# State-space scan: rows of summed decays from a DRAM scratch instead of TensorE spreads

## What is computed

```python
acum = jnp.cumsum(loga, axis=2)            # summed decays, per head
tril = jnp.tril(jnp.ones((CHUNK, CHUNK), dtype=bool))[:, :, None, None]
seg = jnp.exp(jnp.where(tril, acum[:, :, :, None] - acum[:, :, None], -jnp.inf))
cb = jnp.einsum('bcign,bcjgn->bcijg', cm, bm)
y_intra = jnp.einsum('bcijgr,bcjgrp->bcigrp', seg * cb[..., None], v)
cdec = jnp.exp(acum)

def step(s, xc):
    bm_c, wgt_c, v_c, al_c, cm_c, cd_c = xc
    y = jnp.einsum('bign,bgrnp->bigrp', cm_c, s) * cd_c[..., None]
    return advance(s, bm_c, wgt_c, v_c, al_c), y
```

## Time and profile before

| | us |
|---|---|
| median of 3 runs | 2179.41 (2177.7 to 2180.89) |
| the profiled execution | 2180.74, its span 2179.0 |
| TensorE busy | 1892.8 (87%) |
| VectorE, ScalarE, GpSimd busy | 801.6, 508.6, 333.6 |
| the scan, as shown below | 440.3 to 536.7 |

### The profile page before, as it was taken

One profiled execution on the slowest core, in us unless ns is written; L12 is line 12 of the kernel. 1 busy time (PEld: TensorE's weight loads), 2 busy tenths in 40 slices (PEclk: granted clock), 3 DMA queues, 4 the chain that ended last, 5 costly groups with the idle time before them and its releaser, 6 DMA issues.

```text
span 2179.0 us, 32920 instructions
## 1 busy us (share of the span) xinstructions
PE 1892.8 (87%) x14024; PEld 1133.5 (52%) x14024; DVE 801.6 (37%) x1427; ACT 508.6 (23%) x1119; POOL 333.6 (15%) x323
## 2 busy tenths in 40 slices
PE   6999989999999989888899999989999976656566
PEld 3874668845875433333236566578887731212112
DVE  3331757655543010000026877667764300000001
ACT  2452321343012100001023323444442100000001
POOL 1431044422320000000013000045540000000000
PEclk9999999999999999999999999999999987888878
DMA  9321051230239999999993433300004699999997
GB/s 385 142 87 77 2 196 78 102 131 1 96 146 394 429 429 427 429 430 430 430 403 133 188 155 117 127 2 2 3 2 184 235 430 429 428 430 429 432 431 294
DMA packets 46690, 528.07 MB, mean 242 GB/s; under 512 B 3409, under 2 KB 7761, under 8 KB 23121
## 3 DMA queue, kind: packets, MB, share of 16 engines
q1 hardware_dynamic: 44784, 522.56, 57.5%
q10 hardware_dynamic: 1760, 3.42, 0.4%
HBM read 524.91 MB, written 1.05 MB: 241 GB/s over the span
## 4 chain that ended last, share of the span: by engine, by line
PE 54%; DMA 28%; DVE 11%; issue 2%; ACT 2%; DVEq 1%; POOLq 1%; POOL 0%; ACTq 0%; PEld 0%; SPq 0%; PEldq 0%
DMA ring<-in_moe_w 27%; PE bank L1442 12%; PE bank L711 8%; PE bank L822 7%; PE bank L1324 4%; PE bank L1257 3%; PE bank L790 3%; DVE x L2285 2%; PE bank L1020 2%; PE bank L1043 2%; DMA ring<-in_mod_w 1%; DVE x L2877 1%; PE bank L965 1%; DVE ring L2414 1%; PE bank L629 1%
## 5 line engine op out<-in xcount | busy, mean ns | idle before, releaser
L1442 PE MATMUL bank<-ring,xgs 128*32 128x512 f32 x2984 | 377.4, 660 | 128.1 <-DMA ring<-in_moe_w 126.8
L1442 PEld LDWEIGHTS bank<-ring,xgs 128*32 128x32 f32 x2984 | 106.8, 120 | 372.3 <-issue 287.1
L1442 PE MATMUL bank<-ring,hT 128*32 128x512 f32 x1488 | 198.9, 689 | 67.5 <-DMA ring<-in_moe_w 67.5
L822 PE MATMUL bank<-hT,ring 128*128 128x256 f32 (+1 forms) x784 | 232.7, 454 | 2.0 <-ACT hT L1612 1.4
L2718 DVE SCALAR_TENSOR_TENSOR x<-bank,modT,x 128x256 f32<-128x256 f32 x96 | 42.4, 480 | 456.9 <-PE bank L1466 456.7
L822 PEld LDWEIGHTS bank<-hT,ring 128*128 128x128 f32 x784 | 146.6, 190 | 82.3 <-issue 66.8
L1442 PEld LDWEIGHTS bank<-ring,hT 128*32 128x32 f32 x1488 | 54.0, 124 | 198.5 <-issue 149.2
L2285 DVE SCALAR_TENSOR_TENSOR x<-gluR,cols,x 128x256 f32<-128x256 f32 x240 | 116.2, 484 | 16.6 <-issue 0.9
L711 PE MATMUL bank<-hT,ring 128*128 128x256 f32 x432 | 99.9, 381 | 4.2 <-ACT ssd_g L1663 2.2
L711 PEld LDWEIGHTS bank<-hT,ring 128*128 128x128 f32 x432 | 81.1, 190 | 18.2 <-issue 6.3
L3109 POOL MEMSET gluR<- 128x3008 f32 x1 | 2.6, 2611 | 500.0 <-DVEq L2728 500.0
(11 more groups left out here) (578 smaller groups left out, 3057.2 us busy)
## 6 DMA issues: line engine op xcount, KB each, us to landing
ring<-in_moe_w SPq DMA_DIRECT2D x56, 4096.0 KB, 22.6
ring<-in_moe_w SPq DMA_DIRECT2D x28, 2048.0 KB, 20.9
ring<-in_moe_w SPq DMA_DIRECT2D x55, 1024.0 KB, 14.6
ring<-in_mod_w SPq DMA_DIRECT2D x12, 4096.0 KB, 13.5
ring<-in_moe_w SPq DMA_DIRECT2D x12, 3072.0 KB, 21.9
ring<-in_cd_w SPq DMA_DIRECT2D x6, 4096.0 KB, 14.1
ring<-in_ab_w SPq DMA_DIRECT2D x5, 4096.0 KB, 19.5
ring<-in_ab_wo SPq DMA_DIRECT2D x2, 4096.0 KB, 13.9
```

The source lines that it names most:

```text
L822: last = mm(ps[p["no"] % 4][:, p["c0"]:T], w[:, k, :], hT[:, k, p["c0"]:T], start=(k == 0), stop=(k == KD - 1))
L1442: last = mm(ps[banks + s][32 * j:32 * j + 32, :], lhs[s][:, 4 * kh + k, 32 * j:32 * j + 32], piece(g, k, j), start=(kh == 0 and k == 0), s ...
```

## The change

The rows of `ac` are written once to a DRAM scratch (`rows_out`), and each row comes back by a DMA whose source repeats it for 128 partitions, straight into the matrix buffer (`decay_rows`; two per pair and direction, on SP's queue, among the weight loads). The spread and mask products and their constants go. So that no exponential overflows where j lies beyond i, the matrices hp = 1 ("far") take |ac_j - ac_i| on ScalarE, and hp = 0 ("near") the minimum with ac_j on VectorE (`bounded`); the mask, now a factor 0 or 1 (`past`), goes into the C-B product, which is kept per direction. The order of matrices is by direction first; TensorE counts `ssd_y` twice a pair, when direction 0 and when direction 1 has been multiplied. The first four broadcast pairs (k = 0, 1) stand in SP's order ahead of the load `about` 4, the other twelve ahead of `mod10` 0.

```diff
+        def rows_out(sp):
+
+            sp.wait_ge(sg("gate_cums"), 1)
+            sp.dma_start(ssd_rows, ac[64:128, :]).then_inc(sg("dram_written"), 16)
+            sp.wait_ge(sg("dram_written"), 16)
+            sp.wait_ge(sg("gate_cums_turned"), 1)
+
+        def decay_rows(sp, k, d):
+
+            if k >= 2:
+                sp.wait_ge(sg("ssd_y"), 2 * k - 3 + d)
+            for hp in range(2):
+                r = 32 * d + 2 * k + hp
+                sp.dma_start(mats[(4 * k + 2 * d + hp) % 8], ssd_rows[r:r + 1, :].broadcast_to([P, T])).then_inc(sg(f"ssd_row{2 * (k % 2) + d}"), 16)
...
+                if (stage, i) == ("about", 4):
+                    rows_out(sp)
+                    for k in range(2):
+                        for d in range(2):
+                            decay_rows(sp, k, d)
+                if (stage, i) == ("mod10", 0):
+                    for k in range(2, 8):
+                        for d in range(2):
+                            decay_rows(sp, k, d)
                 if n >= RING:
                     sp.wait_ge(w_used, n - RING + 1)
                 load_group(sp, n, stage, i)
...
-                for g in range(2):
-                    dve.wait_ge(sg("ssd_cb"), g + 1)
-                    V.tensor_copy(cbs[g], ps[4 + g]).then_inc(sg("ssd_cbm"), 1)
                 dve.wait_ge(sg("gate_cums_turned"), 1)
...
                 V.tensor_tensor(dtw[:, :, :], ps[2][:, 0:256].rearrange("p (t r) -> p t r", t=NT), acT[:, :, :], ALU.subtract).then_inc(sg("gate_gap"), 1)
+                for g in range(2):
+                    for d in range(2):
+                        V.tensor_tensor(cbs[g][d].rearrange("p (t i) -> p t i", t=NT), ps[4 + g].rearrange("p (t i) -> p t i", t=NT),
+                                        past[:, d:d + 1, :].broadcast_to([P, NT, P]), ALU.mult)
                 dve.wait_ge(sg("gate_exps"), 1)
...
             def ssd():
+                act.wait_ge(sg("ssd_weights"), 1)
                 for k in range(8):
-                    for hp in range(2):
-                        for d in range(2):
-                            u, r = 4 * k + 2 * hp + d, 32 * d + 2 * k + hp
-                            act.wait_ge(sg("ssd_bc"), u + 1)
-                            if k >= 2:
-                                act.wait_ge(sg("ssd_y"), k - 1)
-                            for t in range(NT):
-                                last = A_(mats[u % 8][:, t * P:t * P + P], ps[(4, 5, 7)[u % 3]][:, t * P:t * P + P], ACT.Exp,
-                                          bias=nacT[:, t, r:r + 1])
-                            last.then_inc(sg("ssd_decay"), 1)
+                    for d in range(2):
+                        act.wait_ge(sg(f"ssd_row{2 * (k % 2) + d}"), 32 * (k // 2 + 1))
+                        u, r = 4 * k + 2 * d, 32 * d + 2 * k
+                        far, near = [[mats[(u + hp) % 8][:, t * P:t * P + P] for t in range(NT)] for hp in (1, 0)]
+                        for t in range(NT):
+                            A_(far[t], far[t], ACT.Abs, bias=acT[:, t, r + 1:r + 2], scale=-1.0)
+                        act.drain()
+                        for t in range(NT):
+                            last = A_(far[t], far[t], ACT.Exp, bias=albuf[:, t, r + 1:r + 2], scale=-1.0)
+                        last.then_inc(sg("ssd_decay"), 1)
+                        act.wait_ge(sg("ssd_bounded"), 2 * k + d + 1)
+                        for t in range(NT):
+                            last = A_(near[t], near[t], ACT.Exp, bias=nacT[:, t, r:r + 1])
+                        last.then_inc(sg("ssd_decay"), 1)
...
-                def matrices(k, hp):
+                def matrices(k, d):
...
+                    u = 4 * k + 2 * d
+                    for n, hp in enumerate((1, 0)):
+                        dve.wait_ge(sg("ssd_decay"), u + n + 1)
+                        V.tensor_tensor(mats[(u + hp) % 8], mats[(u + hp) % 8], cbs[k // 4][d], ALU.mult).then_inc(sg("ssd_mat"), 1)
+
+                def bounded(k, d):
...
+                    m, r = mats[(4 * k + 2 * d) % 8].rearrange("p (t i) -> p t i", t=NT), 32 * d + 2 * k
+                    dve.wait_ge(sg(f"ssd_row{2 * (k % 2) + d}"), 32 * (k // 2 + 1))
+                    V.tensor_tensor(m, m, acT[:, :, r:r + 1].broadcast_to([P, NT, P]), ALU.min).then_inc(sg("ssd_bounded"), 1)
...
                     if q in (1, 2):
-                        matrices(k + 1, q - 1)
+                        bounded(k + 1, q - 1)
+                    if q == 3:
+                        matrices(k + 1, 0)
+                    if q == 0 and k >= 0:
+                        matrices(k, 1)
                     if z - 1 in SSD_KV:
                         item_scale(SSD_KV[z - 1])
```

More of the change, by code:

```diff
@@ L166, in hybrid_backbone @@
         ones = sb("ones", [P, P])
-        m_far = sb("m_far", [P, 2, P], BF16)
-        identb = sb("identb", [P, P], BF16)
+        past = sb("past", [P, 2, P])
         rst64 = sb("rst64", [P, T])
@@ L324, in sg @@
             return S[name]
+        ssd_rows = nc.dram_tensor("ssd_rows", (64, T), F32, kind="Internal").ap()
         block = ctx.enter_context(nc.Block())
@@ L362, in load_experts @@
             if layer == 0:
-                sp.wait_ge(sg("ssd_y"), 8)
+                sp.wait_ge(sg("ssd_y"), 16)
                 sp.dma_start(early[:, :], part(last, 0, 4096)).then_inc(early_in, 16)
@@ L598, in _ @@
                 sp.dma_start(out.rearrange("(k p) t -> p k t", p=P)[:, 4 * half:4 * half + 4, :],
-                             hT[:, 4 * half:4 * half + 4, SEQ:T]).then_inc(sg("out_written"), 16)
-            sp.wait_ge(sg("out_written"), 32)
+                             hT[:, 4 * half:4 * half + 4, SEQ:T]).then_inc(sg("dram_written"), 16)
+            sp.wait_ge(sg("dram_written"), 48)
         @block.tensor
@@ L960, in outputs @@
                         if kind and t == 0:
-                            pe.wait_ge(sg("ssd_mat"), 4 * k + 2 + kind)
+                            pe.wait_ge(sg("ssd_mat"), 4 * k + 2 * kind)
                         for hp in range(2):
                             half = slice(64 * hp, 64 * hp + 64)
-                            right = mats[(4 * k + 2 * hp + kind - 1) % 8][:, tiles[t]] if kind else dskI[:, 2 * k + hp, :]
+                            right = mats[(4 * k + 2 * kind - 2 + hp) % 8][:, tiles[t]] if kind else dskI[:, 2 * k + hp, :]
                             last = mm(ps[k % 4][half, tiles[t]], xs_t[:, k, t, half], right, start=False, stop=True,
                                       skip_group_check=True, tile_position=(0, 64 * hp))
+                        if n == 7:
+                            last.then_inc(sg("ssd_y"), 1)
                     if q == 3:
@@ L987, in ssd @@
                         square_sum(z - 28)
+                pe.wait_ge(sg("mod_added"), 3)
                 for c in range(4, 7):
@@ L2604, in out_projection_ab @@
                 dve.drain().then_inc(sg("pair_out"), 1)
-                dve.wait_ge(sg("x_again"), 16)
+                dve.wait_ge(consts_in, 96)
                 for v in range(4):
@@ L2795, in over @@
                     return v[:, t, r0:r0 + 8].rearrange("p (c a) -> p c a", a=2).unsqueeze(3).broadcast_to([P, 4, 2, 64])
-                def matrices(k, hp):
+                def matrices(k, d):
                     if k >= 8:
                         return
[L2801 to L2804, removed]
+                    u = 4 * k + 2 * d
[3 more added lines that the diff above has]
+                def bounded(k, d):
+                    if k >= 8:
+                        return
+                    m, r = mats[(4 * k + 2 * d) % 8].rearrange("p (t i) -> p t i", t=NT), 32 * d + 2 * k
+                    dve.wait_ge(sg(f"ssd_row{2 * (k % 2) + d}"), 32 * (k // 2 + 1))
+                    V.tensor_tensor(m, m, acT[:, :, r:r + 1].broadcast_to([P, NT, P]), ALU.min).then_inc(sg("ssd_bounded"), 1)
                 def item_state(v):
@@ L2828, in gate @@
                     dve.wait_ge(sg("ssd_acc"), 6 * (c // 4 + 1))
-                    dve.wait_ge(sg("ssd_y"), c + 1)
+                    dve.wait_ge(sg("ssd_y"), 2 * c + 2)
                     V.tensor_tensor(zmix[:, c, :], zmix[:, c, :], ps[c % 4], ALU.mult).then_inc(sg("ssd_gated"), 1)
@@ L2947, in _ @@
             G.memset(ones[:, :], 1.0)
-            G.memset(identb[:, :], 0.0)
-            G.memset(m_far[:, :, :], 0.0)
+            G.memset(past[:, :, :], 1.0)
             G.memset(m_gla[:, :, :], 1)
@@ L2958, in _ @@
                             pattern=[[-1, P]], channel_multiplier=1)
-            G.affine_select(out=identb[:, :], in_=identb[:, :], compare_op=ALU.not_equal, fill=1.0, base=0,
-                            pattern=[[-1, P]], channel_multiplier=1)
             for d in range(2):
                 sign = 1 - 2 * d
-                G.affine_select(out=m_far[:, d, :], in_=m_far[:, d, :], compare_op=ALU.is_ge, fill=-1e30, base=0,
```

(3 more changed lines are left out.)

11 lines of the change are left out of this document (3 added, 8 removed).

## The result

| | runs | median us | ratio to before (95%) |
|---|---|---|---|
| before | 8 | 2179.27 | |
| changed | 8 | 2186.05 | 1.0026 (1.0017 to 1.0035) |
| changed, second set | 10 | 2184.65 | 1.0021 (1.0012 to 1.0031) |

The forecast was 2168 in a range from 2160.5 to 2177: the sign is wrong, and some 18 us lie between forecast and measurement. The profiled execution took 2181.81 us and is the quickest of its eight; the second profile (2188.53) is the slowest of its ten.

What follows compares the result with a forecast made beforehand. TensorE was taken to pace the scan: 25.6 us removed, less 1.5 start, 5.7 gaps, 1.4 VectorE order and 5.0 followers, gains 12.0. From 2180.74, less 1.3 more, 2167.4, stated as 2168; range 2160.5 to 2177.

Steps and rivals of the forecast that it cites:

- Gaps laid open: Scan's item chain: six gaps after inter products, formerly covered by spread blocks, give back 0.95 us each, 5.7 in all.
- Where the followers overtake TensorE: Scan: TensorE waits at kv(7) 1.5 us, add(6) 1.7 and the squares at z = 28 1.8; together 5.0.
- VectorE. ... Order matters more: VectorE's queue in the scan: added work fits except before item_scale(1), 0.6 us, and beside GpSimd's skip block, 0.8; together 1.4.
- Removed: TensorE in the scan: 16 spread blocks of 1.60 us each disappear, 25.6 us.
- only TensorE and the bare gaps count: Rival for the scan: rows early, ScalarE never behind, gain 18.9 us, time 2160.5; chance 0.12.
- Start: Start of the scan: waiting for GpSimd's weighting and the new first minimum loses 1.0 and 0.5 us, together 1.5.
- ScalarE: Scan: twelve activations per direction and k at 0.27 us plus 0.2 for the drain, 3.5 us, 16 times 56.
- rival 3: ScalarE reloads its table at every Abs/Exp change: 5 us slower, with stalls about 2186; chance 0.09 including other losses.
- Minima: VectorE in the scan: 16 added minima, 0.68 us each or 0.60 back to back, 10 us in all.
- Transfers: Row broadcasts for the scan land 2.9 us from issue, 3.3 a pair; delayed weight loads still arrive before use.
- rival 2: Scan: ScalarE or the row broadcasts bind more, 2172 to 2179 us, moderate case 2173; chance 0.17.
- Masked copies: ssd_gates on VectorE: four copies instead of two stay hidden behind ScalarE's table load; uncovered they would cost 2.4 us.

Runs made afterwards that it cites:

- warm at the start only: Changed kernel plus ident-by-ident products on TensorE only around the modulation row's turn and at steps -2 and 0; 2182.27 us, ratio 0.9996 to before.
- without spreads: Kernel of before with its spread and mask products removed and nothing put in their place (matrices not computed); 2169.03 us, ratio 0.9947 to before.
- fewer ident products: Changed kernel with GpSimd's mixings held, pair 3's gate earlier and fewer gap-filling ident products than that best version; 2170.78 us, ratio 0.9948 to before.

## Why the prediction was wrong

**The step that failed** is the pricing of idle time in "Gaps laid open" and in "Where the followers overtake TensorE". Each gap was priced at its own length, 0.95 us six times and 5.0 at three later places, with the products between at the durations of a kernel whose clock never fell. The experiments show that the gaps also bring TensorE to its lower clock: products that keep it busy inside the same gaps give back 6.9 us alone (0.9986 against 1.0021), and 0.9957 against 1.0002 with the collision gone. The Trainium skill ("TensorE: Matmul & The Clock Gate", section on a second HAM failure mode) describes a kernel that idles briefly between groups of products and goes back and forth between the two clocks; the traces here agree, and I had not weighed it. The profile's sign was there to be read: the earlier trace rows show TensorE busy 93% of the stage, and the forecast itself put it at 64 of 84 us.

**The second step** is "VectorE. ... Order matters more". The walk met GpSimd's skip block and charged 0.8, but it did not look for what else GpSimd does while the matrices move to later steps. The mixings ran from 507.6 before as well, beside no multiplication of matrices. Their price was 3.9 us alone (1.0002 against 1.0021), and 0.9957 against 0.9986 with the clock held. The Trainium skill ("SBUF — State Buffer", section "SBUF: two separate sides") says that VectorE with two SBUF inputs and GpSimd share a port pair as an exclusive lock held for an instruction, so that the other blocks. The trace agrees: each mixing took about 2.8 us, so the first ended near 507.5, and the multiplication of 2.84 us that began at 505.24 ended at 508.08, some 0.6 behind it.

Of the 18 us between forecast and measurement these two steps hold about 14. With both held, the kernel gains 9 to 10 us against the 12.0 of the sum, and its scan takes 89.8 us where the walk gives 524.7 - 438.8 = 85.9. The rest of the working, term by term:

- *Removed:* 25.6 us of products are gone, as counted. But removal alone shortens the scan by 9.0 us, so "only TensorE and the bare gaps count" was never near. TensorE is busy 76.1 us in the changed scan and not near 64, since part of its products ran at the lower clock.
- *Start:* the first kv product comes 2.59 us behind the copy's start instead of 3.20; 0.6 gained as worked out, and given back by the clock (1.63 us for 1.10).
- *Gaps:* the six that were priced at 0.95 measured 0.87, 1.92, 0.85, 0.94, 5.12 and 0.85 us (steps 0, 4, 8, 17, 21, 25): four as said, one behind GpSimd's skip block (1.0 more, priced at 0.8 under VectorE), one behind the mixings. Steps 15 and 23 had a bare gap before as well, which the forecast does not name; no term hangs on it.
- *ScalarE:* no table load stands between Abs and Exp; rival 3's mechanism is out, though its sign came true. The three sets of four, timeline of ScalarE:

```profile
484.56 1.26 ACT L2005 ACTIVATE x<-x,ssd_g 128x128 f32<-128x128 f32 x4
485.89 1.28 ACT L2008 ACTIVATE x<-x,ssd_g 128x128 f32<-128x128 f32 x4
487.07 1.26 ACT L2012 ACTIVATE x<-x,ssd_g 128x128 f32<-128x128 f32 x4
488.24 1.26 ACT L2005 ACTIVATE x<-x,ssd_g 128x128 f32<-128x128 f32 x4
```

  484.56 to 488.24 is 3.68 us a direction and k against 3.5; a set of four starts 1.18 us behind the last, 0.29 each and not 0.27.
- *Minima:* 0.68 us, as taken from the earlier trace rows.
- *Transfers:* 3.6 us to landing against 2.9, up to 6.7 for single ones, where the forecast had called over 6 a sign of being wrong; the write 2.3. Waits of ScalarE and VectorE for rows sum to 6.8 us in the whole scan, and the changed chain contains two of them (3.52 and 4.68 us of DMA). That is part of rival 2, "the rows bind more". Of the loads behind them, the second of `ab_wo` was issued at 436.47; `mod10` part 0 came at 522.8 instead of near 509, still long before its use.
- *Followers overtake:* `matrices(3,1)` held TensorE 2.5 us (forecast 1.5), the gate of pair 3 1.6 (1.7), the squares 3.0 (1.8). The places were right, the sizes at two of them too small.
- *Masked copies:* hidden; VectorE waited 0.39 us more for ScalarE behind them.

Rival 3 had the sign right by luck: it forecast 2186 for a reason that the trace denies.

Open: how much of the 2 to 4 us of the followers' new work is ScalarE's and how much VectorE's, why the falls differ in depth between executions, and why the same wait of 1.92 us goes with a fall in one kernel and not in the other. The clock is known here only by the granted clock beside these waits.

## What to carry to other kernels

Before taking work from an engine that paces a stage, write down what that work covers: here 25.6 us of products hid the gaps of a serial chain, and their removal alone shortened the scan by 9.0. If the stage is left with TensorE idle between short groups, work out too what it costs if the products that follow run at the lower clock, and try cheap products in the gaps before giving up a change. When instructions of VectorE move in time, look up what GpSimd does at the new place.

## What the hardware showed

- In the changed kernel TensorE's granted clock fell to half behind two waits of 1.5 and 1.3 us (437 to 440), and behind waits of 1.9 (near 463), 2.5 (near 485) and 3.0 us (near 530), not only behind the one of 5.1. None of these lengths decides alone: it read 1.00 behind the same 1.9 us in the kernel warm at the start only, behind the same 1.5 and 1.3 us in the kernel without spreads (TensorE busy for 2.86 and 2.25 us of the windows from 435 and 440, the fall only from 445), and in the kernel with fewer ident products where TensorE was busy for 3.04 us of 5.
- Adding 83 small products to the changed kernel, 22.3 us of busy TensorE in the profile, made it 6.9 us faster.
- A multiplication of VectorE with both inputs in SBUF took 2.84 us beside a GpSimd operation on SBUF and 0.68 without, and the two GpSimd operations took 5.54 against 4.66.
- A 2 KB row repeated to 128 partitions from DRAM landed 3.0 to 6.7 us after its issue, 3.6 in the median.
